# Query and z projections by the seven-product scheme, cut in halves between the steps of a scan, with the decay differences on ScalarE

## The reference, cut to what matters

```python
proj = hn @ w_in                       # (256, 1024) @ (1024, D_IN_PROJ)
z, xbc, dt_raw, q, k, v, qi, ki, wi, g_ssd, g_attn = jnp.split(proj, splits, axis=-1)
# the scan, chunks of L = 128 tokens, per group g of 8 heads:
acum = jnp.cumsum(dtc * a_neg, axis=1)
seg = acum[:, :, None] - acum[:, None, :]
decay = jnp.exp(jnp.where(causal, seg, -jnp.inf))
cb = jnp.einsum('btgn,bsgn->btsg', cc, bc)
y_diag = jnp.einsum('btsg,btsgh,bsghp->btghp', cb, decay, xdt)
# after the scan:
y = y.reshape(Bsz, S, SSD_D_INNER) * jax.nn.silu(z.astype(F32))
# the attention's queries:
q = apply_rope(q.reshape(Bsz, S, ATTN_HEADS, ATTN_HEAD_DIM), cos_a, sin_a)
```

## Time and profile before

| | |
|---|---|
| median of 3 runs | 1572.61 us (1572.56 to 1574.87) |
| the profiled execution's own time | 1573.15 us |
| its span, first to last instruction | 1571.3 us |
| mean granted TensorE clock | 0.971 of full speed |
| PE busy | 1428.7 us (91%) |
| DVE busy | 734.7 us (47%) |
| ACT busy | 356.9 us (23%) |
| DMA | 350.00 MB, mean 223 GB/s |

### The profile page before, as it was taken

One profiled execution on the slowest core, in us unless ns is written; L12 is line 12 of the kernel. 1 busy time (PEld: TensorE's weight loads), 2 busy tenths in 40 slices (PEclk: granted clock), 3 DMA queues, 4 the chain that ended last, 5 costly groups with the idle time before them and its releaser, 6 DMA issues.

```text
span 1571.3 us, 22447 instructions
## 1 busy us (share of the span) xinstructions
PE 1428.7 (91%) x9140; PEld 1044.5 (66%) x9140; DVE 734.7 (47%) x1550; ACT 356.9 (23%) x702; POOL 66.8 (4%) x64
## 2 busy tenths in 40 slices
PE   7999999999999987777699999999999999787684
PEld 5885667899998554334268856588999985444241
DVE  3473446666975341111135734575779743321122
ACT  2221546501111121001122224473011021110010
POOL 0000420000000000000000013200000000000000
PEclk9999999999999998889999999999999999998898
DMA  8443233336641679999963442232464417999996
GB/s 297 159 148 121 107 108 108 107 89 254 225 161 56 267 305 378 419 417 416 395 228 120 148 161 80 81 111 104 158 248 164 170 45 301 368 376 418 415 417 260
DMA packets 115703, 350.00 MB, mean 223 GB/s; under 512 B 11665, under 2 KB 13969, under 8 KB 99217
## 3 DMA queue, kind: packets, MB, share of 16 engines
q1 hardware_dynamic: 114912, 345.95, 57.6%
q0 software_dynamic: 688, 2.62, 0.4%
HBM read 347.50 MB, written 1.05 MB: 222 GB/s over the span
## 4 chain that ended last, share of the span: by engine, by line
PE 47%; issue 15%; DMA 7%; DVE 2%; ACT 0%; SPq 0%; DVEq 0%; POOL 0%; POOLq 0%
PE bank L797 10%; PE bank L748 10%; PE bank L767 9%; DMA ga<-in_w_down_e 6%; PE bank L800 5%; PE bank L1078 2%; PE bank L1107 2%; PE bank L724 2%; DMA wring<-in_w_up_e 1%; PE bank L1150 1%; PE bank L1003 1%; PE bank L914 1%; PE bank L1133 1%; PE bank L990 0%; PE bank L903 0%
## 5 line engine op out<-in xcount | busy, mean ns | idle before, releaser
L767 PE MATMUL bank<-hT,wring 128*128 128x256 f32 x1280 | 281.9, 380 | 0.0
L767 PEld LDWEIGHTS bank<-hT,wring 128*128 128x128 f32 x1280 | 241.3, 190 | 35.9 <-issue 3.3
L748 PE MATMUL bank<-wring,hT 128*128 128x512 f32 (+2 forms) x576 | 217.5, 534 | 0.0
L1107 PE MATMUL bank<-wring,big 128*32 128x256 f32 x2048 | 141.5, 438 | 58.8 <-DMA wring<-in_w_up_e 41.1
L748 PEld LDWEIGHTS bank<-wring,hT 128*128 128x128 f32 x576 | 104.5, 191 | 105.3 <-issue 103.3
L1107 PEld LDWEIGHTS bank<-wring,big 128*32 128x32 f32 x2048 | 71.4, 125 | 127.2 <-DMA wring<-in_w_up_e 45.0
L1946 DVE TENSOR_TENSOR h<-bank,h 128x512 f32<-128x512 f32 x64 | 44.2, 691 | 113.0 <-PE bank L1150 113.0
L1546 DVE SCALAR_TENSOR_TENSOR scr<-bank,prm,scr 128x255 f32<-128x255 f32 (+1 forms) x144 | 62.7, 477 | 58.3 <-ACT scr L1205 55.6
L1078 PE MATMUL bank<-big,xn 128*128 128x256 f32 x256 | 74.6, 454 | 14.8 <-DVE big L1864 14.8
L1939 DVE TENSOR_TENSOR big<-bank,big 128x256 f32<-128x256 f32 x16 | 6.8, 425 | 166.5 <-ACT big L1351 166.5
L1078 PEld LDWEIGHTS bank<-big,xn 128*128 128x128 f32 x256 | 67.3, 335 | 24.4 <-DVE big L1864 19.7
(11 more groups left out here) (299 smaller groups left out, 1951.7 us busy)
## 6 DMA issues: line engine op xcount, KB each, us to landing
wring<-in_w_in SPq DMA_DIRECT2D x68, 1024.0 KB, 7.0
wring<-in_w_gate_e SPq DMA_DIRECT2D x16, 4096.0 KB, 20.2
wring<-in_w_up_e SPq DMA_DIRECT2D x16, 4096.0 KB, 21.2
wring<-in_w_ssd_o SPq DMA_DIRECT2D x16, 1024.0 KB, 6.2
wring<-in_w_ckv SPq DMA_DIRECT2D x16, 1024.0 KB, 7.5
scr<-in_w_down_e SPq DMA_DIRECT2D x8, 2048.0 KB, 28.4
ga<-in_w_down_e SPq DMA_DIRECT2D x8, 2048.0 KB, 30.1
qq<-in_w_down_e SPq DMA_DIRECT2D x8, 2048.0 KB, 25.8
```

The costliest lines, as they stand in the source:

```text
L748: ins = nc.tensor.matmul(bank[bank_of(job)][:, 0:width], src[:, k, t * P:(t + 1) * P], wring[:, SLOT[c], k, 0:width], start=i == 0, stop=i ...
L767: ins = nc.tensor.matmul(bank[bank_of(job)][:, i * SEQ:(i + 1) * SEQ], wring[:, SLOT[c], k, m:m + P], src[:, k, :], start=n == 0, stop=n = ...
L1107: ins = nc.tensor.matmul(bank[b][j * S:(j + 1) * S, i * F:(i + 1) * F], xg[:, k, e:e + S], up_part[i][:, j, k * F:(k + 1) * F], start=k == ...
```

## The change

Queries and z go by the seven-product scheme. The list gains `("sums", "h0")` between the fifth and the sixth xbc chunk: DVE makes the four sums of quarters of the normalised input there, and the first two weight sums of the first q chunk. A q chunk is a whole unit: seven products, then `join` (the parts of `combine`, in two halves) writes the quarters to `qbuf`, and the rotation is done in place from there. A z chunk is split over two scan steps: products 1, 2, 5 and 6 in the even step, 3, 7 and 4 in the odd one. Its sums on DVE (`join` of a half) come a step later in the list, ahead of the scan's results of that step. z's Silu is no longer taken from the bank: DVE writes the sums to `zt`, and ACT does the Silu in place, for chunks 0 and 1 at step 6 and for chunks 2 and 3 after the scan (`zsilu`).

The decay differences move from DVE to ACT: a Relu of (acum - difference) out of the bank and Exp with scale -1 in place of DVE's subtraction and minimum. DVE keeps the product with the masked scores (`mask`), which now stands at the end of the step's list. A few buffers move: the scan's `ytmp` to the place of `xdtt`, the early chunks' temporaries to parts of `mix` and `att`, the weight sums to the lower half of `ga`, the input sums to `xn`.

```diff
-    o += [("idx", 1, i) for i in range(2)] + [("topk", 1), ("xbc", 3), ("xbc", 4), ("xbc", 5)]
+    o += [("idx", 1, i) for i in range(2)] + [("topk", 1), ("xbc", 3), ("xbc", 4), ("sums", "h0"), ("xbc", 5)]
...
     for n, (t, g) in enumerate(SSD):
         o += [("decay", n)]
         if n:
-            o += [("ssd", n - 1)]
-        o += [("part", ("z", n // 2), n % 2)]
+            o += [("join", ("z", (n - 1) // 2), (n - 1) % 2), ("ssd", n - 1)]
+        o += [("part", ("z", n // 2), n % 2), ("mask", n)]
         if n in (1, 3):
             o += [("qT", n - 1), ("qT", n)]
-    o += [("ssd", len(SSD) - 1)]
+        if n == len(SSD) - 2:
+            o += [("zsilu", 0), ("zsilu", 1)]
+    o += [("join", ("z", 3), 1), ("ssd", len(SSD) - 1), ("zsilu", 2), ("zsilu", 3)]
...
+SEVEN = {"q": "h0", "z": "h0", "ssdo": "y", "atto": "att", "wo": "merged", "ck": "mem", "cv": "mem", "cq": "h"}
 PRODUCTS = (1, 2, 5, 6, 3, 7, 4)
+HALVES = (PRODUCTS[:4], PRODUCTS[4:])
...
-                    by_token(l, st[1], hT, tiles=st[2:3])
+                    seven(l, st[1], {}, products=HALVES[st[2]])
+                elif kind == "q":
+                    seven(l, st, {})
...
+            def join(l, st, half, put):
+
+                prod1, prod5, part2, part3, part4 = temps(st)
+                if half == 0:
+                    weight_sums(l, st, (3,))
+                    job, b = product(l, st, 2)
+                    drained(dve, l, JOB[(st, 1)])
+                    drain_inc(put(0, 0, b, prod1, ALU.add), job)
+                    job, b = product(l, st, 6)
+                    drain_inc(V.tensor_tensor(part2, b, prod1, ALU.add), job)
+                    drained(dve, l, job)
+                    drained(dve, l, JOB[(st, 5)])
+                    link(V.tensor_tensor(part4, part2, prod5, ALU.add))
+                    weight_sums(l, st, (4,))
+                    return
+                job, b = product(l, st, 3)
+                drain_inc(put(0, 1, b, part4, ALU.add), job)
+                after = UNITS[UNITS.index(st) + 1]
+                if after[0] in EARLY:
+                    weight_sums(l, after, (1, 2))
+                job, b = product(l, st, 7)
+                drain_inc(V.tensor_tensor(part3, b, part2, ALU.add), job)
+                drained(dve, l, job)
+                link(put(1, 1, part3, prod5, ALU.add))
+                job, b = product(l, st, 4)
+                drain_inc(put(1, 0, part3, b, ALU.subtract), job)
...
-                    drain_inc(nc.scalar.activation(zt[:, t, n:n + NCOL], bank[bank_of(job)][:, :], ACT.Silu), job)
+                elif kind == "zsilu":
+
+                    n = st[1] * NCOL
+                    drained(act, l, JOB[(("z", st[1]), 4)])
+                    for t in range(TT):
+                        ins = nc.scalar.activation(zt[:, t, n:n + NCOL], zt[:, t, n:n + NCOL], ACT.Silu)
+                    ins.then_inc(z_rdy, 1)
...
                 elif kind == "decay":
...
-                    act.wait_ge(seg_rdy, l * len(SSD) + (n + 1))
-                    nc.scalar.activation(mm_[:, n % 2, :], mm_[:, n % 2, :], ACT.Exp).then_inc(dec_rdy, 1)
+                        for i in range(4):
+                            hd = 4 * j + i
+                            ins = nc.scalar.activation(mm_[:, n % 2, hd * P:(hd + 1) * P], bank[bank_of(job)][:, i * P:(i + 1) * P],
+                                                       ACT.Relu, bias=acum[:, t, g * HG + hd:g * HG + hd + 1], scale=-1.0)
+                        drain_inc(ins, job)
+                    drained(act, l, job)
+                    nc.scalar.activation(mm_[:, n % 2, :], mm_[:, n % 2, :], ACT.Exp, scale=-1.0).then_inc(dec_rdy, 1)
...
+                elif kind == "mask":
...
                     dve.wait_ge(dec_rdy, l * len(SSD) + (n + 1))
                     m3 = mm_[:, n % 2, :].rearrange("p (h t) -> p h t", h=HG)
                     V.tensor_tensor(m3, m3, bc(cbm[:, t, g * P:(g + 1) * P], 1, HG), ALU.mult).then_inc(m_rdy, 1)
```

More of the change, by code:

```diff
@@ L170, in make_jobs @@
             jobs += [(st, p, "act" if p in (1, 5) else "dve") for p in PRODUCTS]
+        elif st[0] == "part" and st[1][0] in SEVEN:
+            jobs += [(st[1], p, "act" if p in (1, 5) else "dve") for p in HALVES[st[2]]]
         elif st[0] == "part":
@@ L770, in by_channel, with seven @@
                     ins.then_inc(filled_s, 1)
-            def seven(l, st, made, by_channel=False):
-                for i in range(CHUNKED[st[0]]):
-                    chunk_in(l, CHUNK[(st, i)])
+            def seven(l, st, made, by_channel=False, products=PRODUCTS):
+                if products[0] == PRODUCTS[0]:
+                    for i in range(CHUNKED[st[0]]):
+                        chunk_in(l, CHUNK[(st, i)])
                 w11, w12, w21, w22 = weight_quarters(st)
@@ L1170, in _, with products_1_and_5 @@
             steps = Steps(act, a_step)
+            def products_1_and_5(l, st):
+                u = UNITS.index(st)
+                prod1, prod5 = temps(st)[:2]
+                for p, to, read in ((1, prod1, 6), (5, prod5, 4)):
+                    filled(act, l, JOB[(st, p)])
+                    if u:
+                        drained(act, l, JOB[(UNITS[u - 1], read)])
+                    drain_inc(nc.scalar.activation(to, bank[bank_of(JOB[(st, p)])][:, 0:HALF_W], ACT.Copy), JOB[(st, p)])
             def stage(l, st):
@@ L1431, in weight_sums, with product @@
                     V.tensor_tensor(out, a, b, ALU.subtract).then_inc(wsum_rdy, 1)
+            def product(l, st, p):
+                job = JOB[(st, p)]
+                filled(dve, l, job)
+                return job, bank[bank_of(job)][:, 0:HALF_W]
+            def join(l, st, half, put):
[23 more added lines that the diff above has]
+                drain_inc(put(1, 0, part3, b, ALU.subtract), job)
             def combine(l, st, put):
@@ L1528, in stage, with put @@
                         filled(dve, l, job)
-                        n = NCOL * st[1] if kind == "q" else 0
-                        if kind == "q" and st[1] == 0 and t == 0:
-                            filled(dve, l, JOB[(("qiT", 1), 0)])
-                        dst = qbuf[:, t, n:n + NCOL].rearrange("p (h d) -> p h d", d=HD)
+                        dst = qbuf[:, t, 0:NCOL].rearrange("p (h d) -> p h d", d=HD)
                         link(rope(bank[bank_of(job)][:, :], NCOL // HD, t, dst))
                         drain_inc(dve.nop(), job)
+                elif kind == "q":
+                    n = NCOL * st[1]
+                    def put(a, b, x, y, op):
+                        return V.tensor_tensor(qbuf[:, a, n + b * HALF_W:n + (b + 1) * HALF_W], x, y, op)
+                    for half in range(2):
+                        join(l, st, half, put)
+                    drained(dve, l, JOB[(st, 4)])
+                    for t in range(TT):
+                        src = qbuf[:, t, n:n + NCOL]
+                        link(rope(src, NCOL // HD, t, src.rearrange("p (h d) -> p h d", d=HD), rel[:, 0, :], rel[:, 1, :]))
+                    dve.nop().then_inc(q_rdy, 1)
+                elif kind == "join":
+                    _, of, half = st
+                    def put(a, b, x, y, op):
+                        n = of[1] * NCOL + b * HALF_W
+                        return V.tensor_tensor(zt[:, a, n:n + HALF_W], x, y, op)
+                    join(l, of, half, put)
                 elif kind == "xbc":
```

91 lines of the change are left out of this document (45 added, 46 removed).

## The result

| | before | after |
|---|---|---|
| median | 1573.46 us (1572.56 to 1574.87, 4 runs) | 1552.9 us (1552.55 to 1554.5, 4 runs) |
| span of the profiled execution | 1571.3 us | 1550.4 us |
| granted TensorE clock | 0.971 | 0.971 |
| PE busy | 1428.7 us | 1407.3 us |

The ratio is 0.9871, with a 95% interval of 0.9853 to 0.9888: 1.3% faster. The forecast was 1553.5 us.

A forecast was written before the change was run, and what follows sets the result against it. The prediction took PE's own queue to bound the changed windows. From 1573.15 us it took 19.7 us of PE work, added 0.6 us of waiting, and allowed 0.54 us for the median: 1553.5 us, range 1550 to 1563.

The forecast's parts named there:

- PE's work: In q and z chunks: seven products save 1.64 us a chunk, 12 chunks, 19.7 us.
- rival C: In the seven-product chunks: the weight loads show, 18.6 us a chunk, 1632 us; chance 1%.
- The steady steps: In the scan's step pairs: DVE's 16.4 us fit in PE's 19.13, with mask product margins of 4.3 and 2.6 us.
- step 7: At the last mask product, behind ACT's work: 0.3 us of waiting in each layer, bounds 0 and 1.7 us.
- rival A: At the odd scan steps: DVE or ACT late, 11 us of the gain lost, 1565 us; chance 12%.
- rival B: Ahead of each scan product: PE waits for the mask product, DVE and POOL lengthening each other, 1578 us; chance 5%.
- The first q chunk: Ahead of this chunk: DVE's four input and two weight sums, 5.2 us, end at 122.8 and cost nothing.
- the first mask product: At scan step 0: done by T + 7.3 (7.9 beside POOL), wanted by PE at T + 8.65; no wait.
- T: The start of a scan step's decay stage, from which the prediction counts times in us.
- ACT's total: Over the kernel: 24 table loads go, 128 Relus and 24 copies come, +28 us busy, near 385 us.
- The sum: Whole kernel: 1573.15 - 19.7 + 0.6 = 1554.05 us, with the runs' median 0.54 us lower: 1553.5 us.
- Rival D: In the expert stage, bound by DMA in part: half the gain given back as waiting, 1563 us; chance 4%.

The follow-up runs named there:

- dose_2_after: The changed kernel with two unused DVE maxima over 128x1024 (1.22 us each) in each scan step, behind the mask product: 1556.27 us.
- sub_on_dve_but_first: The changed kernel with the decay subtractions back on DVE, except those of step 0, which stay on ACT: 1553.1 us.
- sums_in_same_step: The changed kernel with the sums of a z half in their own step, ahead of the mask product, not a step later: 1615.26 us.
- silu_two_tables: The changed kernel with an unused one-column Exp between the Silu pairs at step 6, so ACT loads its table twice more: 1563.19 us.
- sub_on_dve: The changed kernel with the decay subtractions of all steps back on DVE, between the half's sums and the scan's results: 1562.29 us.
- dose_4_after: The changed kernel with four unused DVE maxima over 128x1024 in each scan step, behind the mask product: 1590.22 us.

## Why the prediction was right

**PE's work.** Right: a z pair of 19.12 us (19.13 said), a q chunk of 12.09 (12.1 said), PE busy 1407.3 (1409 said). The 28 loads of a chunk stay hidden: 56 records in 12.09 us (125.78 to 137.87), 0.216 us each. So rival C is out, and the rule of the Trainium skill ("TensorE: Matmul & The Clock Gate", What overlaps and what doesn't) that would have made this change lose does not hold for these loads, all of which use the whole array. Leaving q out gives its share back (1559.96).

**The steady steps.** Right in what matters, with DVE's time too high: 14 us a pair against 16.4 said. Of that 0.9 us were waits, which busy time doesn't hold; the rest is that the sum adds up record lengths, and the records of operations in a row overlap (see step 7). Over the whole kernel DVE is busy 811.8 us, somewhat more than the 800 said. The margins are real: some four microseconds more a pair fit in most pairs (dose_2_after), and rival A's waits did not come. A chain like rival B's can be made: the kernel with the sums in the same step has it, by its order and not by POOL, and there it costs more than B's price.

**The first q chunk and the first mask product.** The sums ahead of the first q chunk stand where they were said to: DVE has them done at 122.73 (122.8 said), and PE does not wait. At the first mask product the outcome, no wait, was right, and the working was not. These are DVE's and POOL's rows after:

```profile
155.44 1.41 DVE L1552 TENSOR_TENSOR scr<-qq,cst 128x512 f32<-128x512 f32 x1
156.78 1.53 DVE L1553 TENSOR_TENSOR scr<-qq,cst 128x512 f32<-128x512 f32 x1
158.34 1.15 DVE L1555 TENSOR_TENSOR qq<-scr 128x256 f32<-128x256 f32 x1
159.41 1.26 DVE L1556 TENSOR_TENSOR qq<-scr 128x256 f32<-128x256 f32 x1
160.89 1.29 DVE L1705 TENSOR_TENSOR mix<-bank,cst 128x512 f32<-128x512 f32 x2 [0.21 <-DVE qq L1556]
162.21 1.23 DVE L1715 TENSOR_TENSOR scr<-scr,mix 128x1024 f32<-128x1024 f32 x1
```

```profile
154.98 1.32 POOL L706 TENSOR_TENSOR ga<-xs,dtb 128x512 f32<-128x512 f32 x1 [129.26 <-ACT xs L1273]
156.38 1.37 POOL L712 TENSOR_TENSOR ga<-ga,tail 128x512 f32<-128x512 f32 x1
```

The prediction gave the rotation its old 0.69 and 0.42 us. But the rotation now reads `qbuf`, no longer a bank, so both inputs of all its operations are in SBUF, and its second tile runs while POOL works: 5.35 us in place of the 2.2 that the first tile takes just before. DVE is free for the mask product at T + 6.5, where T + 3.1 was said, and is done at 163.44; PE wants it at 164.33. The margin was 0.9 us and not the 1.35 worked out, and the working had taken ACT for the late engine: DVE came 3.4 us later than said and ACT 0.8 us earlier. That the two errors left a margin was luck. How narrow it is the kernel with the subtractions on DVE shows: 2.15 us of subtractions and 1.25 us of waiting for the Exp behind them, and PE waits. This is what the move to ACT is for, and only in step 0 (sub_on_dve_but_first).

**Step 7.** The step that failed: 0.3 us of waiting a layer was forecast, and there was none. ACT's rows:

```profile
222.75 2.19 ACT L1297 ACTIVATE big<-big 128x512 f32<-128x512 f32 x4
224.85 2.15 ACT L1324 ACTIVATE scr<-bank,acum 128x128 f32<-128x128 f32 x8
227.02 1.28 ACT L1328 ACT_TABLE_LOAD   x1
228.31 1.06 ACT L1328 ACTIVATE scr<-scr 128x1024 f32<-128x1024 f32 x1
```

Eight Relus take 2.15 us, 0.27 each, where 0.39 was taken and 0.28 was the lower bound. All of them by shape (busy us, mean ns of one, idle before):

```profile
L1324 ACT ACTIVATE scr<-bank,acum 128x128 f32<-128x128 f32 x128 | 34.8, 387 | 24.8 <-PE bank L924 24.8
```

So the 0.39 us taken from the score's Exp was right for one record. What was wrong is the sum 8 x 0.39: in a row the records start 0.25 us apart and overlap, and 128 of them hold ACT for 34.8 us, not for 49.9. The lower bound came near by luck, since it was worked out as the length of one record. The rows before held the warning: the subtractions' row shows 128 records with a mean of 342 ns and 34.5 us of busy time, 0.27 us each. With this spacing the mask product ends at 230.71 and PE wants it at 231.28. The same term explains ACT's total: 15 us less, 369.0 busy where 385 was said.

**The sum.** 1553.5 said, 1552.9 measured. PE's work gave the 19.7 us forecast (19.8), the 0.6 us of waiting did not come, and the untouched stages were 1.1 us shorter in the profiled execution, which is within what runs of one kernel differ by. Rival D is out: from the cross-attention's first value chunk of layer 0 to the first q chunk of layer 1, the expert stage included, it is 452.6 us (441.05 to 893.65) where it was 452.8 (451.98 to 904.78), so nothing was given back.

## What to carry to other kernels

Where one engine sets the time, count its queue, and then measure the slack of the others at their narrowest place, not over a stage: here 4 us of spare DVE time a pair went with 0.9 us at one product. Before work is moved off an engine, look for the single place where it is late; one step in eight was enough. When you add up a row of short operations, take the row's busy time divided by its count, not the mean length of one. And price a wait of the matmul engine above its length, since the granted clock may fall behind it.

## What was not expected of the hardware

- Behind many PE waits of 1.3 to 2.55 us, in a stretch that is otherwise full, groups run at the 1.2 GHz level in place of 2.4 for a while (a 128x512 pair of records in 2.02 us in place of 1.08). How often and for how long varied between waits of one length:

| waits | how many, in which kernels | behind them |
|---|---|---|
| 2.54 to 2.55 us | 8, sums_in_same_step | 1.8 to 3.5 us more each |
| 2.29 to 2.32 us | 4, silu_two_tables and sub_on_dve | 1.7, 3.3, 1.7 and 0.1 us more |
| 1.34 to 1.93 us | 3 in sums_in_same_step, 10 in dose_4_after | 7 of 13 followed by slow groups |
| 1.09 to 1.27 us | 3 in sums_in_same_step, 2 in dose_2_after, 1 in dose_4_after | the usual times |

  With four doses a group of 1.89 us took 3.68 behind a wait of 1.93 (171.49) in layer 0; behind the same wait in layer 1 (957.80) it took 1.99. What decides between them no run here shows.
- DVE operations with two inputs, both in SBUF, and POOL's operations in the scan stretch each other: 0.69 to 1.53 us (128x512), 1.22 to 2.06 (128x1024), POOL's 128x512 from 1.04 to 2.02. Sums with an input in a bank kept their 0.42 us beside POOL, and the doses, with one input in SBUF, their 1.2 (two of them in 2.46 us from 191.46 on, dose_2_after). DVE's rows after, and POOL's:

```profile
169.33 0.41 DVE L1630 TENSOR_TENSOR big<-bank,ga 128x256 f32<-128x256 f32 x1
169.67 1.73 DVE L1475 TENSOR_TENSOR ga<-wring 128x1024 f32<-128x1024 f32 x1
171.43 1.95 DVE L1475 TENSOR_TENSOR ga<-wring,ga 128x1024 f32<-128x1024 f32 x1
```

```profile
168.29 2.02 POOL L714 TENSOR_TENSOR xs<-xs,prm 128x512 f32<-128x512 f32 x1
170.27 2.02 POOL L706 TENSOR_TENSOR ga<-xs,dtb 128x512 f32<-128x512 f32 x1
```
